# Block 2's SiLUs and last convolution tap on ScalarE, VectorE with three taps, and a new table of places

## The reference

```python
GDN_CONV = 4                      # causal, one weight per channel and tap
# q, k and v of the delta rule, 512 channels each, 256 tokens:
#   y[t] = silu(w[0]*x[t-3] + w[1]*x[t-2] + w[2]*x[t-1] + w[3]*x[t])
y_mla  = mla_mixer(...) * jax.nn.silu(m_gate)
y_gdn  = gdn_mixer(g_q, g_k, g_v, g_z, g_b, g_a, ...)   # its output is gated by silu(g_z)
y_moba = moba_mixer(c_q, c_k, c_v, t5_table) * jax.nn.silu(c_gate)
return x + jnp.concatenate([y_mla, y_gdn, y_moba], axis=-1) @ w_out
```

## Time and profile before

| | |
|---|---|
| time, median of 3 runs | 1423.34 us (1422.61 to 1423.68) |
| time of the profiled execution | 1429.22 us |
| its span, first to last instruction | 1427.4 us |
| PE busy | 1374.8 us (96%) |
| DVE busy | 1072.4 us (75%) |
| ACT busy | 746.6 us (52%) |
| POOL busy | 68.0 us (5%) |
| mean granted TensorE clock | 0.989 |

### The profile page before, as it was taken

The page is one execution under the profiler, slowest core; times in us unless marked ns, Lnnn a source line. Parts: engine busy times, 40 slices in busy tenths (PEclk is TensorE's granted clock), DMA queues, the critical chain, the costliest instruction groups (busy, mean ns, idle before and its releaser), DMA issues.

```text
span 1427.4 us, 25394 instructions
## 1 busy us (share of the span) xinstructions
PE 1374.8 (96%) x10226; PEld 1294.3 (91%) x10226; DVE 1072.4 (75%) x1844; ACT 746.6 (52%) x1145; POOL 68.0 (5%) x62
## 2 busy tenths in 40 slices
PE   7999999999999999999999999999989999979998
PEld 6899999998999988999999989999878999879996
DVE  6899898667766777998986777666778657687556
ACT  6454656555444554546565555444564436654344
POOL 0000000000000000000000000000001210002210
PEclk9999999999999999999999999999989999979999
DMA  7565354565565555554445655564542114431122
GB/s 269 177 205 179 120 169 155 177 209 172 180 206 181 176 162 201 188 168 148 148 164 162 207 178 179 206 204 156 194 152 75 45 60 149 155 118 60 60 89 74
DMA packets 108844, 223.89 MB, mean 157 GB/s; under 512 B 6036, under 2 KB 17556, under 8 KB 108600
## 3 DMA queue, kind: packets, MB, share of 16 engines
q1 hardware_dynamic: 106352, 218.93, 46.3%
q10 hardware_dynamic: 2376, 3.35, 0.7%
HBM read 221.21 MB, written 1.06 MB: 156 GB/s over the span
## 4 chain that ended last, share of the span: by engine, by line
PE 41%; DVE 5%; ACT 2%; issue 1%; DMA 1%; DVEq 0%; ACTq 0%; POOLq 0%; POOL 0%
PE bank L481 13%; PE bank L456 8%; PE bank L490 7%; PE bank L503 6%; PE bank L511 2%; PE bank L461 2%; DVE w L2241 2%; DVE wlo L1714 1%; ACT whi L1140 1%; PE bank L526 1%; PE bank L1108 1%; DMA ring<-in_w_in 1%; PE bank L1111 1%; PE bank L533 0%; DVE w L2238 0%
## 5 line engine op out<-in xcount | busy, mean ns | idle before, releaser
L1714 DVE TENSOR_TENSOR wlo<-ring,whi 128x1024 fp32r<-128x1024 f32 (+3 forms) x430 | 500.4, 1186 | 191.8 <-ACT whi L1140 168.9
L1140 ACT ACTIVATE whi<-ring 128x1024 fp32r<-128x1024 f32 (+3 forms) x430 | 433.8, 1026 | 376.2 <-PE bank L481 237.5
L481 PE MATMUL bank<-hhi,whi 128*128 128x256 f32 x2016 | 281.2, 281 | 7.1 <-ACT sgb L1398 4.8
L490 PE MATMUL bank<-hhi,wlo 128*128 128x256 f32 x2016 | 280.7, 281 | 0.0
L481 PE MATMUL bank<-hlo,whi 128*128 128x256 f32 x2016 | 276.5, 279 | 0.0
L481 PEld LDWEIGHTS bank<-hhi,whi 128*128 128x128 f32 x2016 | 254.7, 189 | 11.6 <-ACT sgb L1398 5.5
L490 PEld LDWEIGHTS bank<-hhi,wlo 128*128 128x128 f32 x2016 | 253.9, 190 | 1.9 <-issue 1.3
L481 PEld LDWEIGHTS bank<-hlo,whi 128*128 128x128 f32 x2016 | 252.8, 189 | 0.0
L456 PE MATMUL bank<-w 128*128 128x128 f32 (+5 forms) x928 | 132.1, 295 | 0.0
L456 PEld LDWEIGHTS bank<-w 128*128 128x128 f32 (+2 forms) x928 | 116.3, 192 | 7.4 <-issue 1.8
L503 PE MATMUL bank<-whi,hhi 128*128 128x512 f32 (+2 forms) x256 | 99.4, 390 | 0.0
(11 more groups left out here) (301 smaller groups left out, 1570.8 us busy)
## 6 DMA issues: line engine op xcount, KB each, us to landing
ring<-in_w_in SPq DMA_DIRECT2D x100, 1024.0 KB, 5.1
ring<-in_w_ffn_down SPq DMA_DIRECT2D x22, 1024.0 KB, 5.0
ring<-in_w_ffn_gate SPq DMA_DIRECT2D x20, 1024.0 KB, 5.1
ring<-in_w_ffn_up SPq DMA_DIRECT2D x20, 1024.0 KB, 5.1
ring<-in_w_merge SPq DMA_DIRECT2D x8, 1024.0 KB, 4.9
ring<-in_w_out SPq DMA_DIRECT2D x8, 1024.0 KB, 5.1
ring<-in_w_oc SPq DMA_DIRECT2D x4, 1024.0 KB, 5.1
ring<-in_w_od SPq DMA_DIRECT2D x4, 1024.0 KB, 5.0
```

Source lines behind the costliest of these rows:

```text
L481: done = e.matmul(o, wh[:, k, cols(u)], s_[:, k0 + k, :], stop=False, skip_group_check=True, start=opens and k == 0 and s_ is sh and u % 2 ...
L490: done = e.matmul(o, wl[:, k, cols(u)], sh[:, k0 + k, :], start=False, stop=closes, skip_group_check=True)
L1140: e.activation(part_of(whi, j), part_raw(j), ACT.Copy).then_inc(*up("hi.a"))
L1714: e.tensor_tensor(part_of(wlo, j), part_raw(j), part_of(whi, j), ALU.subtract).then_inc(*up("lo.v"))
```

## The change

The last tap goes to ScalarE: beside the copy into `gdp`, four activations of 128 x 256 for each of kc, qc and vc read the bank and write bank times weight into the result (`kc`, `qc`, `vc`). VectorE adds the three other taps to it. All SiLUs are ScalarE's Silu: in place on kc, qc and vc, and straight from the banks for cg, mg and z. VectorE's products with `sgb` go, and so do ScalarE's waits that kept `sgb` safe. `taps` has three steps instead of six, and the table is new for all tasks.

```diff
 TWO_PLAN = {
-        "taps": [11, 11, 22, 26, 34, 35],
+        "taps": [12, 22, 34],
-        "decay": [10, 10, 17, 17],
+        "decay": [10, 10, 11, 12],
...
             def taps_a(l):
                 for i, tag in enumerate(("kc", "qc", "vc")):
-                    yield 2 * i
+                    yield i
                     for p_ in range(2):
+                        d2 = flat((kc, qc, vc)[i][:, 2 * p_:2 * p_ + 2])
                         e.wait_ge(*at("taps", l, tag, p_))
-                        if i and p_ == 0:
-                            e.wait_ge(*at(("kc", "qc")[i - 1], l))
-                        e.activation(flat(sgb[:, 2 * p_:2 * p_ + 2]), flat((kc, qc, vc)[i][:, 2 * p_:2 * p_ + 2]),
-                                     ACT.Sigmoid).then_inc(*up("taps.a"))
-                        put("taps.a", "tsig", l, tag, p_)
+                        e.activation(d2, d2, ACT.Silu).then_inc(*up("taps.a"))
+                        put("taps.a", tag, "half", l, p_)
+                    put("taps.a", tag, l)
...
-                def silu_a(i, *key):
-                    bk = bank(*key)
-                    e.activation(flat(sgb[:, 2 * i:2 * i + 2]), bk[:, :], ACT.Sigmoid).then_inc(*up("two.a"))
-                    put("two.a", "silu", *key)
+                def silu_a(dst, *key):
+                    e.activation(flat(dst), bank(*key)[:, :], ACT.Silu).then_inc(*up("two.a"))
+                    leave("two.a", *key)
...
                             e.activation(gdp[:, i, :, 3:259], two(bk[:, :]), ACT.Copy).then_inc(*up("two.a"))
+                            n = ("kc", "qc", "vc").index(name)
+                            for u in range(2):
+                                c = 2 * i + u
+                                wc = 4 * ((4, 0, 8)[n] + c) + 3
+                                e.activation((kc, qc, vc)[n][:, c], bk[:, u * S:u * S + S], ACT.Copy,
+                                             scale=prm("gdn_w", l, wc, wc + 1)).then_inc(*up("two.a"))
                             put("two.a", "gdp", l, name, i)
...
-                last = [None] * 2
-                e.wait_ge(*at("gdp", l, tag, p_))
-                for k4 in range(4):
+                last = [at("gdp", l, tag, p_)] * 2
+                for k4 in range(3):
                     for u in range(2):
...
-                    yield 2 * i + 1
-                    for p_ in range(2):
-                        d2 = flat((kc, qc, vc)[i][:, 2 * p_:2 * p_ + 2])
-                        e.wait_ge(*at("tsig", l, tag, p_))
-                        e.tensor_tensor(d2, d2, flat(sgb[:, 2 * p_:2 * p_ + 2]), ALU.mult).then_inc(*up("taps.v"))
...
-                def silu_v(dst, i, *key):
-                    bk = bank(*key)
-                    e.wait_ge(*at("silu", *key))
-                    e.tensor_tensor(flat(dst), bk[:, :], flat(sgb[:, 2 * i:2 * i + 2]), ALU.mult).then_inc(*up("two.v"))
-                    leave("two.v", *key)
```

More of the change, by code:

```diff
@@ L92 @@
 TWO_PLAN = {
-        "bias": [6, 6, 21, 21],
-        "taps": [11, 11, 22, 26, 34, 35],
-        "others": [27, 34, 42, 48, 50],
-        "decay": [10, 10, 17, 17],
-        "delta": [21, 23, 23, 23, 26, 29, 37, 38, 39, 40, 42, 45, 46, 47, 47, 47, 48, 49, 51, 52, 52, 55, 58, 66, 67],
-        "latent": [26, 29, 31, 31, 36, 37, 39, 41, 43, 44, 52, 61, 64],
-        "outs": [59, 66, 67, 67],
+        "bias": [5, 5, 16, 20],
+        "taps": [12, 22, 34],
+        "others": [28, 33, 41, 42, 44],
+        "decay": [10, 10, 11, 12],
+        "delta": [21, 22, 22, 23, 26, 32, 37, 38, 39, 40, 41, 41, 44, 45, 45, 45, 48, 50, 51, 52, 53, 57, 60, 68, 69],
+        "latent": [26, 29, 31, 31, 35, 37, 39, 42, 43, 43, 55, 62, 64],
+        "outs": [58, 66, 70, 75],
 }
@@ L1665, in two_a @@
                         put("two.a", "cv", l)
[L1666 to L1667 removed]
+                        silu_a(cgs, "cg", l)
+                        put("two.a", "cgs", l)
                     elif name == "mg":
                         e.wait_ge(*at(name, "done", l))
[L1670 removed]
+                        silu_a(mgs, "mg", l, 0)
+                        put("two.a", "mgs", l)
                 if l == L - 1:
@@ L1674, in two_a @@
                 e.wait_ge(*at("z", "done", l))
-                e.wait_ge(*at("mgs", l))
                 for i in range(2):
-                    silu_a(i, "z", l, i)
+                    silu_a(zs[:, 2 * i:2 * i + 2], "z", l, i)
+                put("two.a", "zs", l)
                 for i in range(6):
@@ L2236, in four_taps @@
                         wv = prm("gdn_w", l, (c0 + c) * 4 + k4, (c0 + c) * 4 + k4 + 1)
[L2237 to L2242, removed]
+                        e.wait_ge(*last[u])
+                        e.scalar_tensor_tensor(out=dst[:, c], in0=gdp[:, p_, u, k4:k4 + S], scalar=wv, in1=dst[:, c],
+                                               op0=ALU.mult, op1=ALU.add).then_inc(*up("taps.v"))
                         last[u] = now("taps.v")
@@ L2246, in taps_v @@
             def taps_v(l):
-                for i, tag in enumerate(("kc", "qc", "vc")):
-                    yield 2 * i
+                for i in range(3):
+                    yield i
                     four_taps(l, i, 1)
-                    yield 2 * i + 1
-                    for p_ in range(2):
-                        d2 = flat((kc, qc, vc)[i][:, 2 * p_:2 * p_ + 2])
-                        e.wait_ge(*at("tsig", l, tag, p_))
-                        e.tensor_tensor(d2, d2, flat(sgb[:, 2 * p_:2 * p_ + 2]), ALU.mult).then_inc(*up("taps.v"))
-                        put("taps.v", tag, "half", l, p_)
-                    put("taps.v", tag, l)
             def decay_v(l):
@@ L2529, in two_v @@
                         four_taps(l, ("kc", "qc", "vc").index(name), 0)
[L2530 to L2538, removed]
                 for i in range(6):
```

## The result

The changed kernel takes 1408.49 us, median of 4 runs (1406.11 to 1412.86); the kernel before, beside it on the same chip, 1422.97 us (1419.92 to 1423.68, 4 runs). The ratio is 0.9891, 95% interval 0.9863 to 0.9920. On a second chip it was 0.9896 (0.9869 to 0.9923). The forecast was 1411 us, range 1402 to 1421, faster with 0.75.

What follows compares the result with a forecast made beforehand. PE, 96% busy, bounds the kernel, so only its idleness and clock loss can be won: 5.4 (front waits) + 5.0 (clock) + 2.0 (later parts) = 12.4 us off 1429.2, 1416.8; median 5.9 below, 1411; range 1402 to 1421.

Steps and rivals of the forecast that it cites:

- (a): Front stretch: kc's scaled copies make ba's rows 1.6 us later; new PE wait of 1.2 us, 0.8 in layer 1.
- (c): Front stretch: PE's sums wait 2.5 us for `gv`, the copies of the sums cost 0.5; the 5.6 us wait goes.
- (d): Front stretch, squares' wait (L1550): qc's copies are 1.6 us longer; 1.0 us in each layer, bounds 0 and 2.6.
- (e): Front stretch: the wait for L2406 falls from 1.7 us to 0.4, that for L2385 from 0.5 to 0.
- Later parts: Behind the front stretch: bank and other waits shrink, vc's longer copies cost some; gain 2 us in all, bounds -3 and 4.7.
- rival D: Slower: ScalarE's in-order queue holds the splits, so PE waits for `whi` in parts 10 to 20; 1430 us, chance 0.11.
- The clock: PE's low-clock loss in block 2: each layer pays 3.9 us; gain 0 in layer 0, 5.0 in layer 1.
- rival B: The clock stays up, since no wait over 2.5 us is left; 7.8 us more off, 1403 us, chance 0.17.
- "All of the answer lies": Claim that the front stretch (parts 5 to 13) of both layers costs 29 us beyond PE's work and holds the answer.
- Rival E: The waits only move: sums stand where their producer isn't ready, later parts gain nothing; 1423 us, chance 0.09.
- A: The main forecast of 1411 us, own range 1406 to 1417, chance 0.50.
- C: Three gaps within 9 us bring one long low-clock stretch in both layers; 9.9 us less gain, 1421 us, chance 0.13.

Runs made afterwards that it cites:

- its repetition: The changed kernel run once more, unchanged, on a second chip; ratio to the kernel before 0.9896 (0.9869 to 0.9923).
- the tap back: The changed kernel, but VectorE makes all four taps and ScalarE's 24 scaled copies are gone; table and Silu stay; ratio to the kernel before 0.9933.
- The run with 39 loads: The changed kernel with kc's second taps at place 13 instead of 12, so kc's SiLU stands behind Dm's exponentials; ratio to the kernel before 0.9939.

## Why the prediction was right

**The size.** Forecast 12.4 us off the profiled execution, then 5.9 for the median: 1411, measured 1408.5. Over the two profiles block 2 is 19.4 us shorter. In windows of 1 us that is 10.5 us of idleness, 7.9 of clock and 1.0 of rest; the prediction had 7.4 (5.4 + 2.0) and 5.0. So the mechanism was the forecast one (the long wait goes, a shorter one on `gv` comes, some clock is won back), but by these two profiles its sum of 12.4 us was 7 us too small, in the waits of the front stretch and in the clock. That 1411 lies 2.5 us from the median is therefore partly luck. The profiled execution of before lay 5.9 us above the median of its runs, that of after 2.4 below, and the difference of the medians, 14.5 us, is what the sum came near.

**(a) ba's rows**: 1.2 and 0.8 us of new wait were predicted, 0 and 0.2 came. The scaled copies did push the rows back, by 1.4 us against kc's first copy (3.3 us from 1032.16 to 1035.49; before 1.9). But the prediction held PE fixed against ScalarE, and it isn't. In layer 0, from the split ahead of kc's copies, which waits for the landing of weights (3.02 us here), to ba's product it is 3.65 us in the profile of before, 5.36 in after, 4.8 in its repetition and also 4.8 with before's code and the new table, 4.3 with the tap back. A distance that differs by 0.6 us between two runs of the same kernel, and by up to 1.7 between kernels, was taken as given to a tenth. With the copies doubled no such distance was enough, and the wait was there, 1.4 us.

**(c) `gv`**: 2.5 us each, measured 1.95 and 2.57. The chain to `gv` was well reckoned: its end was forecast 8.7 us behind the start of that split, and it came at 8.6. When PE comes there was luck: forecast were 3.65 us and a wait of 1.2 on ba's rows, 4.85 together, and PE came to ba's product after 5.36 without a wait; the two errors nearly cancel. "Copies of the sums" came out at 0 rather than 0.5, since PE was at the lower clock just there: its first products of part 6 took 3.2 us from 1040.60 to the start of the spreading at 1043.76, where 1.9 was counted; with 1.9 PE would have been there 0.6 us before the copies were done (1043.03). The wait is hidden under PE's slowness, and isn't a gain.

**(d), (e)**: 1.6 against 2.0 and 1.0 against 0.8; in all 7.3 us of waits are left in the front stretch, where 10.8 was forecast, so 8.9 us gained and not 5.4.

**Later parts**: 2.0 us were forecast and 1.2 came: the bank waits on L2342 and L1655 went as told (3.5 us), L2433 kept 1.0 of 1.2, and latent's turned heads cost 2.5 us instead of 0.8. There the cause given was wrong. Not the 1.6 us of copies of vc, as the doubled copies show, but a chain: twelve taps in a row on VectorE, L1532's own wait for them, and on ScalarE two SiLUs which wait for them too and stand ahead of a split and of the turned heads. This is the mechanism of rival D, real and small: ScalarE's in-order queue behind a SiLU that waits. It held up the turned heads and not, as D had it, the splits; no product of PE waited for `whi` in block 2 of the changed kernel. It shows once more in the squares' wait, which rises by 2.4 to 4.4 us where kc's SiLU stands late.

**The clock**: 3.9 us a layer were left to it; in the profile it is 3.4 and 1.7, in the repetition 1.7 and 3.4. In all four layers 1.7 of it lies behind the wait on `gv`. The rest in the profile lies in layer 0's first products (1017 to 1021), in the repetition behind the squares of layer 1. The waits ahead of these two drops (1.27 and 0.39 us on `xn`; 1.03 on the squares) stand in both profiles, each with a drop behind it in one of them only. So rival B (it stays up) was rightly not the forecast. The words that of the drops only two follow a long wait need an addition: behind `gv` waits of 1.95 and 2.57 us PE fell to half clock about 1 us later in both layers (windows above, 0.66 and 0.83). The Trainium skill (TensorE: Matmul & The Clock Gate, "Why this matters for your kernels") says that gaps of some length between bursts bring the low clock back. Here these gaps were followed by it, while 1.3 us on the turned heads was not: the 5 us windows behind it read 1.00. Rival B had one reading of the earlier trace rows wrong: it says that the two longest drops of layer 0 follow a 5 us wait, but layer 0 has two drops, and the second (1066.95) follows the column sums of the squares, as the paragraph on the clock says.

**Table loads**: 43, eleven a layer in block 2, as forecast; 1.28 us each and no gap behind. The Trainium skill (ScalarE: Activation LUTs, "What ACT_TABLE_LOAD costs") has twice that for a switch, and on the same page ("Table sets: the hidden batching unit") advises grouping by set. The run with 39 loads was grouped better and was not faster, so in this kernel the order by need was worth more; the measurement decides. It doesn't say that loads are free: the one ahead of the logarithm stands on the way to `gv`.

**"All of the answer lies"** in the front stretch: of the waits, yes (8.9 of the 10.1 us that the named ones lost). Of the clock, the largest piece is the drop at 1278.32, gone with the 1.7 us wait ahead of it, which is now 0.5; the forecast let layer 1 gain 5.0 us of clock without saying which drop would go.

**Rival E** had 0.09 and describes the run with the table alone (0.9996). What kept it from being the result is VectorE's shorter queue. The prediction had both in its sum but never said that the table is worth nothing without the shorter queue.

**The chances** were added up wrongly. A, B and a third of C make 0.50 + 0.17 + 0.04 = 0.71 for faster, not 0.75, and the rest of C with E makes 0.18 for the same, not 0.14. Neither changes the forecast.

What stays open: whether a version with the sums later and the squares ahead of the splits would beat the changed kernel. None of the four orders tried did. Open too is what decides whether a short wait is followed by the low clock; behind the same waits of the same kernel it came in one profile and not in the other. And no run takes away the table load that stands on the way to `gv`.

## What to carry to other kernels

A step that is placed earlier gains only as far as its producer is ready earlier as well; time the two halves apart before crediting either. After moving work to an engine that is half idle, look at what stands behind each of its instructions that wait, and put the waiting one where the engine would be idle anyway. Table loads that fall into such idleness cost nothing that showed here, and avoiding them by reordering can cost more than they do; a load on the way to what TensorE waits for is another matter. Count TensorE's idle time and what its clock loses together: from one run to the next the one can turn into the other.

## What the runs showed beyond that

The changed kernel spread by 6.75 us over four runs (1406.11 to 1412.86), and the part ahead of block 2, untouched, lay 3.5 us apart in two profiles of it (block 2 began at 1015.4 and 1018.9). PE's idle time there was 22.5 and 21.7 us, and the clock lost 1.5 and 3.3 us, so half of the difference is clock. Inside block 2, early in layer 0, a wait of PE on one small transfer (in_flip), 0 to 2.0 us, comes and goes between runs. A SiLU over 128 x 512 takes 632 ns, as the Sigmoid did, and a scaled copy of 128 x 256 from a bank 485 ns, and two of them 0.83.
